# A mixture-of-experts tail: residual rows added by GpSimd's transfers onto copied bias products

## The reference

```python
act = (up + 1.0) * (gate * jax.nn.sigmoid(SWIGLU_ALPHA * gate))
return act @ w_down[e] + b_down[e]                      # per expert
...
out = jnp.einsum('tkd,tk->td', y_assign.reshape(T, TOP_K, D), gates.astype(h.dtype))
...
x = x + moe_ffn(rms_norm(x, ffn_norm[l]), ...)
return rms_norm(x, final_norm)
```

## Time and profile before

| | us |
|---|---|
| median of 3 runs (lowest, highest) | 2077.31 (2076.71, 2078.88) |
| the profiled execution | 2076.9 |
| its span | 2075.1 |
| PE busy | 1955.7 |
| DVE busy | 1579.5 |
| ACT busy | 1397.3 |
| POOL busy | 468.7 |

### The profile page before, as it was taken

The page is one execution under the profiler, slowest core; times in us unless marked ns, Lnnn a source line. Parts: engine busy times, 40 slices in busy tenths (PEclk is TensorE's granted clock), DMA queues, the critical chain, the costliest instruction groups (busy, mean ns, idle before and its releaser), DMA issues.

```text
span 2075.1 us, 38069 instructions
## 1 busy us (share of the span) xinstructions
PE 1955.7 (94%) x11383; PEld 1521.9 (73%) x11384; DVE 1579.5 (76%) x1990; ACT 1397.3 (67%) x1880; POOL 468.7 (23%) x625
## 2 busy tenths in 40 slices
PE   6989999799949999999999999999999999999994
PEld 5777777688737888877877777877876778576583
DVE  5667677778767899987987877976976878586596
ACT  4667768654316888876876766866875777475484
POOL 1222314556420111111111111111111111021023
PEclk9999999899969999999999999999999999999997
DMA  6110020221249999998998988998997999697695
GB/s 228 41 30 22 23 80 1 102 72 63 94 148 326 350 373 373 375 375 314 360 339 287 343 304 286 371 332 276 360 326 251 314 333 337 233 334 253 218 333 200
DMA packets 249636, 507.49 MB, mean 245 GB/s; under 512 B 44502, under 2 KB 61708, under 8 KB 249324
## 3 DMA queue, kind: packets, MB, share of 16 engines
q1 hardware_dynamic: 233948, 463.25, 62.7%
q0 software_dynamic: 15632, 43.53, 8.2%
HBM read 472.09 MB, written 38.55 MB: 246 GB/s over the span
## 4 chain that ended last, share of the span: by engine, by line
PE 77%; SPq 7%; DVE 5%; DMA 4%; issue 3%; ACT 3%; POOL 1%; ACTq 0%; POOLq 0%; DVEq 0%
PE bank L1152 29%; PE bank L1174 15%; PE bank L896 9%; PE bank L1186 7%; SPq L525 4%; PE bank L1203 3%; PE bank L1001 2%; PE bank L924 2%; SPq L536 2%; PE bank L978 1%; PE bank L1142 1%; PE bank L1120 1%; PE bank L1158 1%; DMA slot_in<-slot_rows 1%; PE bank L966 1%
## 5 line engine op out<-in xcount | busy, mean ns | idle before, releaser
L1995 DVE TENSOR_TENSOR w_low<-gu_w,w_high 128x1024 fp32r<-128x1024 f32 x528 | 618.5, 1220 | 222.8 <-ACT w_high L1519 213.4
L1519 ACT CAST w_high<-gu_w 128x1024 fp32r<-128x1024 f32 x528 | 537.7, 1051 | 240.2 <-PE bank L1174 124.2
L1152 PE MATMUL bank<-w_high,x_high 128*128 128x512 f32 x1056 | 415.9, 394 | 2.2 <-DVE w_low L1995 2.2
L1152 PE MATMUL bank<-w_high,x_low 128*128 128x512 f32 x1056 | 413.7, 392 | 0.0
L1152 PE MATMUL bank<-w_low,x_high 128*128 128x512 f32 x1056 | 413.1, 391 | 0.0
L1995 DVE TENSOR_TENSOR w_low<-dn_w,w_high 128x1024 fp32r<-128x1024 f32 x264 | 315.5, 1226 | 24.2 <-ACT w_high L1519 19.3
L1519 ACT CAST w_high<-dn_w 128x1024 fp32r<-128x1024 f32 x264 | 270.0, 1050 | 24.8 <-PE bank L1152 19.5
L1152 PEld LDWEIGHTS bank<-w_high,x_high 128*128 128x128 f32 x1056 | 198.9, 188 | 45.9 <-DVE w_low L1995 3.0
L1152 PEld LDWEIGHTS bank<-w_high,x_low 128*128 128x128 f32 x1056 | 198.8, 188 | 42.8
L1152 PEld LDWEIGHTS bank<-w_low,x_high 128*128 128x128 f32 x1056 | 198.9, 188 | 42.0
L1174 PE MATMUL bank<-w_high,act_high 128*128 128x512 f32 x528 | 215.5, 408 | 0.0
(11 more groups left out here) (247 smaller groups left out, 3104.1 us busy)
## 6 DMA issues: line engine op xcount, KB each, us to landing
gu_w<-in_w_gate_up SPq DMA_DIRECT2D x528, 512.0 KB, 10.5
dn_w<-in_w_down SPq DMA_DIRECT2D x132, 1024.0 KB, 17.2
w_st<-in_w_in SPq DMA_DIRECT2D x14, 512.0 KB, 3.8
xt<-in_x SPq DMA_DIRECT2D x8, 512.0 KB, 10.2
wo_sb<-in_w_out SPq DMA_DIRECT2D x2, 2048.0 KB, 10.4
x<-in_x SPq DMA_DIRECT2D x8, 512.0 KB, 4.2
residual_rows<-x SPq DMA_DIRECT2D x8, 512.0 KB, 2.6
h_rows<-h SPq DMA_DIRECT2D x8, 512.0 KB, 2.8
```

Of the source, the lines that this page charges most:

```text
L1152: mm = pe.matmul(bank[:, 2 * h + g, :], a[:, k, :], b, start=False, stop=last)
L1519: act.copy(w_high[:, u % RING, :], src).then_inc(high_ready, 1)
L1995: dve.tensor_tensor(w_low[:, u % RING, :], raw, w_high[:, u % RING, :], ALU.subtract).then_inc(split_ready, 1)
```

## The change

In the changed kernel ACT copies the products of the even tiles from their banks to fin, and DVE those of the odd tiles, each as soon as they are ready. GpSimd, not SP, moves residual_rows to fin, with transfers that add onto what stands there. Each waits for the copy of its tile and for the last scatter; at most three are under way, on three semaphores `d_fin`. ACT's square waits for the transfer. DVE's add is gone from its loop. The power operations stay on GpSimd: from the fifth transfer on, that of tile t - 4 stands behind the issue for tile t. The semaphores of the first norm (ssq_done, var_done, rstd_done) count on in place of those of the tail.

```diff
--- before.py
+++ after.py
@@ -266,7 +266,6 @@
         d_empty, d_record, d_pad = sem("d_empty"), sem("d_record"), sem("d_pad")
         d_slot, d_slot_first = sem("d_slot"), sem("d_slot_first")
         d_scatter = sem("d_scatter")
-        d_final = sem("d_final")
         d_out = sem("d_out")
 
         dve_step = sem("dve_step")
@@ -315,8 +314,8 @@
         y_ready = sem("y_ready")
         act_passed, dve_passed, pe_passed, sp_passed, pool_passed = (
             sem("act_passed"), sem("dve_passed"), sem("pe_passed"), sem("sp_passed"), sem("pool_passed"))
-        fb_ready, fin_sum, fin_ssq, fin_var, fin_rstd, fin_ready = (
-            sem("fb_ready"), sem("fin_sum"), sem("fin_ssq"), sem("fin_var"), sem("fin_rstd"), sem("fin_ready"))
+        fb_ready, fb_even, fb_odd, fin_ready = sem("fb_ready"), sem("fb_even"), sem("fb_odd"), sem("fin_ready")
+        d_fin = [sem(f"d_fin{k}") for k in range(3)]
 
 
 
@@ -625,9 +624,6 @@
             for r in range(3):
                 sp.dma_start(bdown_raw[NE * r:NE * r + NE, :], b_down).then_inc(d_tail, 16)
             sp.dma_start(final_bc[:], final_norm.rearrange("(a d) -> a d", a=1).to_broadcast([P, D])).then_inc(d_tail, 16)
-            sp.wait_ge(d_scatter, 32 * n_items + 32)
-            for t in range(NT):
-                sp.dma_start(fin[:, t], acc_dram[t * P:(t + 1) * P, :]).then_inc(d_x[t], 16)
             for t in range(NT):
                 sp.wait_ge(fin_ready, t + 1)
                 sp.dma_start(out[t * P:(t + 1) * P, :], fin[:, t]).then_inc(d_out, 16)
@@ -845,8 +841,17 @@
                 pool.sem_inc(pool_passed, 1)
                 choose(e)
             scatter(n_items - 1, 2 * n_items + 2)
+            pool.wait_ge(d_scatter, 32 * n_items + 32)
+            pool.sem_inc(pool_passed, 1)
             for t in range(NT):
-                rstd(fin_var, t + 1, fin_rstd, col(64 + t), col(56 + t))
+                pool.wait_ge((fb_even, fb_odd)[t % 2], t // 2 + 1)
+                if t >= 3:
+                    pool.wait_ge(d_fin[t % 3], 16 * (t // 3))
+                pool.dma_start(fin[:, t], acc_dram[t * P:(t + 1) * P, :], accum_op=ALU.add).then_inc(d_fin[t % 3], 16)
+                if t >= 4:
+                    rstd(var_done, NT + t - 3, rstd_done, col(64 + t - 4), col(56 + t - 4))
+            for t in range(NT - 4, NT):
+                rstd(var_done, NT + t + 1, rstd_done, col(64 + t), col(56 + t))
             pool.wait_ge(d_gather, 16 * n_items + 16)
             pool.wait_ge(d_gather_over, 16 * n_items + 16)
 
@@ -1264,7 +1269,7 @@
                 if t == 2:
                     pe.wait_ge(y_ready, 2 * n_items + 2)
                 if t >= 4:
-                    pe.wait_ge(fin_sum, t - 3)
+                    pe.wait_ge((fb_even, fb_odd)[t % 2], t // 2 - 1)
                 for half in range(2):
                     mm = pe.matmul(bank[:, 2 * (t % 4) + half, :], GT[:, P * t:P * t + P],
                                    bdown[:, 512 * half:512 * half + 512], start=True, stop=True)
@@ -1620,12 +1625,16 @@
             gated_rows(n_items - 1, tokens_of(n_items - 1))
             act.wait_ge(d_tail, 64)
             act.copy(bdown[:], bdown_raw[:]).then_inc(tail_high, 1)
+            for t in range(0, NT, 2):
+                act.wait_ge(fb_ready, t + 1)
+                act.copy(fin[:, t].rearrange("p (h d) -> p h d", h=2), bank[:, 2 * (t % 4):2 * (t % 4) + 2, :]
+                         ).then_inc(fb_even, 1)
             for t in range(NT):
-                act.wait_ge(fin_sum, t + 1)
+                act.wait_ge(d_fin[t % 3], 16 * (t // 3 + 1))
                 act.activation(xg[:, 0], fin[:, t], ACT.Square, accum_out=col(t)).then_inc(act_step, 1)
                 steps[0] += 1
                 act.wait_ge(act_step, steps[0])
-                act.sem_inc(fin_ssq, 1)
+                act.sem_inc(ssq_done, 1)
 
 
 
@@ -2053,16 +2062,15 @@
             dve.wait_ge(tail_high, 1)
             dve.tensor_tensor(bdown[2 * NE:3 * NE, :], bdown_raw[2 * NE:3 * NE, :], bdown[2 * NE:3 * NE, :], ALU.subtract
                               ).then_inc(tail_split, 1)
+            for t in range(1, NT, 2):
+                dve.wait_ge(fb_ready, t + 1)
+                dve.tensor_copy(fin[:, t].rearrange("p (h d) -> p h d", h=2), bank[:, 2 * (t % 4):2 * (t % 4) + 2, :]
+                                ).then_inc(fb_odd, 1)
             for t in range(NT + 2):
-                if t < NT:
-                    dve.wait_ge(fb_ready, t + 1)
-                    dve.wait_ge(d_x[t], 32)
-                    rows = fin[:, t].rearrange("p (h d) -> p h d", h=2)
-                    dve.tensor_tensor(rows, bank[:, 2 * (t % 4):2 * (t % 4) + 2, :], rows, ALU.add).then_inc(fin_sum, 1)
                 if 1 <= t <= NT:
-                    variance(fin_ssq, t, D, col(56 + t - 1), col(t - 1), fin_var)
+                    variance(ssq_done, NT + t, D, col(56 + t - 1), col(t - 1), var_done)
                 if t >= 2:
-                    dve.wait_ge(fin_rstd, t - 1)
+                    dve.wait_ge(rstd_done, NT + t - 1)
                     dve.scalar_tensor_tensor(fin[:, t - 2], fin[:, t - 2], col(64 + t - 2), final_bc[:], ALU.mult, ALU.mult
                                              ).then_inc(fin_ready, 1)
```

## The result

| | us |
|---|---|
| kernel before, median of 6 runs | 2076.02 |
| changed kernel, median of 6 runs (lowest, highest) | 2085.61 (2084.41, 2086.50) |
| ratio, 95% interval | 1.0048 (1.0034 to 1.0061) |
| predicted | 2087.3, range 2077.5 to 2094.0 |

The change costs 9.6 us against the median of before, by the ratio 7 to 13 us. The prediction said 10.0.

The account below looks back on a forecast made before the run. TensorE bounds the body, DVE the tail before the change; adding transfers would bound it after. From 2050.6, 22.3 of transfers, 4.9 of stores, 0.75 landing and 6.6 behind end at 2085.1, +10.0: 2087.3 us, range 2077.5 to 2094.

Parts of the forecast that it names:

- The rate of an adding transfer: Tail, GpSimd's transfers onto fin: each takes 2.79 us, eight take 22.3 us.
- the scatter's row: Profile stretch where only the scatter ran, at 188 GB/s; it gave 2.79 us per 0.524 MB adding transfer.
- rival 2: Tail: with SBUF as destination an adding transfer takes 2.0 us; +3.8 us, 2081.1 us; chance 0.13.
- Stores ahead of the last landing: Tail: four output stores run before the last adding transfer ends and add 4.9 us of engine time.
- The start: Head of the tail: first adding transfer issued at 2049.35, its bytes moving from 2050.6, 1.25 us later.
- The copies: Products copied to fin end after the scatter lands, first at about 2049.3, so not hidden; price 1.8 us.
- Behind the last landing: End of the tail: square to power 2.15, scaling 1.24, then 3.15 to the end; 6.6 us with hand-over.
- Queue order and window: GpSimd's queue in the tail: three transfers in flight, powers behind waits, still keep the DMA engines full.
- The sum: Tail: bytes from 2050.6, plus 22.3, 4.9 and 0.75, then 6.6, ends at 2085.1, 10.0 us later.
- Rival 1: Tail: adding transfers run at a plain load's rate and DVE's relief shows; -2.3 us, 2075.0 us; chance 0.12.
- break-even: Tail: no loss if the last tile lands by 2068.5, at 1.5 us per transfer, 1.7 with three stores ahead.

Follow-up runs that it names:

- e3: Changed kernel with all stores held until the eighth tile is scaled; tail 51.6 us against 46.7, ratio to the kernel before 1.0067.
- e1: Changed kernel with GpSimd's eight adding transfers as plain copies; tail 37.4 us against 46.7, ratio to the kernel before 1.0015.
- e2: Changed kernel with a semaphore per adding transfer, so all eight can be in flight; tail 45.0 us against 46.7, ratio to the kernel before 1.0048.
- e4: Changed kernel with final_norm's load on another semaphore, so b_down's cast does not wait for it; tail 46.4 us against 46.7, ratio to before 1.0047.
- e5: Changed kernel with stores held until the eighth adding transfer has landed; tail 47.4 us against 46.7, ratio to the kernel before 1.0063.

## Why the prediction was right

Times below count from the mark: 2039.22 in the prediction's sum, 2037.51 in the profile after.

- **The rate of an adding transfer (the step that decides): the right side, the size up to 10% off.** I took 2.79 us from the scatter's row; the first gaps are 2.5 us (landings 2.56, 2.49, 2.48 apart, 202 GB/s). Over seven gaps that is 2.0 us too much in the sum. But in e3, where no store is in the way, the seven gaps take 19.3 us together, 2.76 each, so the 2.5 is the low end. Twice the plain load's 1.33, which the prediction gives as 2.66, lies between the two. It is not half way (2.0 us), as rival 2 had it. Whether the rest against the scatter comes from SBUF as destination or from rows in order instead of indices, no run separates. That the add is the cause is shown by e1, and by the packets in e2.
- **Stores ahead of the last landing: too few.** I had four at 1.2 us, 4.9. First landing 15.6, last 39.3, less seven gaps of 2.5, leaves 6.2 us, nearly five (5.3 by the bytes of q1): 1.3 too little. I had named the fifth as possible. With 2.76 per gap it would be 4.4 us and nothing missing; the split between these two terms is not sharper than that.
- **The start: 0.7 too early.** The first adding transfer was issued 10.0 us after the mark, 10.1 in the sum. But it took 5.6 us to land, where 1.25 + 2.79 + 0.75 make 4.8, so it was there at 15.6 and not at 14.9. A part of that is the issue, which I had put at nothing from the rows of plain transfers: this one took 1.16 us instead of 0.75, and up to 2049.0, 1.5 us behind its start, no byte moved:

```profile
2048.00:2049.00 1.00, 1.00 (x4) 0.71 (x4) 0.52 (x2) 0.95 (x1) 0.88 (x2) 0.50 0.00 0
```

- **The copies.** That they do not hide under the scatter was right. Their price of 1.8 us was wrong as a price: e4 takes 1.1 of it away and gets 0.3 back.
- **Behind the last landing: 7.4 us, not 6.6.** The last power ran beside the scaling of the tile before and took 1.52 us; in the earlier trace rows the two last powers take 2.04 together, so the last one there took only 0.5.
- **Queue order and window:** "keeps the engines full" holds, share 1.05. But it was not free: the pair of profiles of e2 shows 1.7 us, which I had at nothing.

The sum: -2.0 + 1.3 + 0.7 + 0.8 = 0.8 us; the prediction's tail was 45.9 and the measured one is 46.7. The mechanism is the one predicted, but the hit to within 2 us of time is owed in part to luck, to errors of both signs. Rival 1 was priced wrongly. Its mechanism, a free add, was run as e1: not 2.3 us less than before but 1.5 more in the tail. The number of stores ahead of the last landing was right (2.01 MB, 3.8 of them, up to 2066.5). What I had wrong is that the engines would be full: they were 0.85 busy from 2048 to 2058, and the last tile landed 30.1 us after the mark where I had 27.0. So the break-even of 1.5 to 1.7 us per transfer was wrong too: at 1.3 us this kernel is still slower than before.

## What to carry to other kernels

A transfer that adds is not a load that saves an add: here it took twice the DMA engines' time of a plain one (2.5 against 1.3 us per 512 KB), so it pays only where those engines have room and the compute engine does not. In a tail in which loads, stores and a last chain share the engines, count the engines' work first; here starting earlier gave back most of what it won. What a queue's wait holds up includes small operations behind it: a wait ahead of the powers made the tail of one hybrid 1.2 us longer than before, and the same two transfers behind the first powers made it 1.5 us shorter.

## What the runs showed of the hardware that I had not expected

- GpSimd needs longer to issue an adding transfer than a plain one of the same shape: 0.88 to 0.92 us (the first 1.16) against 0.54 to 0.59 (e1).
- The one-column power on GpSimd takes 0.5 to 0.6 us alone, 0.9 right behind the issue of an adding transfer, and 1.5 us where DVE's scaling (two inputs of 128x1024 in SBUF) runs beside it. The Trainium skill, "SBUF — State Buffer", section on who interferes with whom, says that such an instruction holds the read port that GpSimd shares; the rows agree: 2078.32 with 1.52, beside DVE's 1.28 from 2078.16.
- With eight adding transfers queued instead of three, stores beside them got 3.9 in place of 5.3 transfers' worth before the last landing. With eight, the two queues took turns packet for packet (144 and 144 in 3.8 us); with three, GpSimd's queue took only 0.24 of the engines for 1.5 us, although two transfers had been issued. The cause of that is open.
- A transfer's landing can trail its bytes: in e3 and e5 the engines were 0.23 and 0.26 busy in the last 2.5 us before the eighth landing.
